# GpSimd's weight split of 128x1024 is four instructions of 128x256 in place of one

## The chip, the cores and the metric

The kernel runs on one core of a Trainium2 chip. The metric is the device time of one launch in microseconds, lower is better. An execution is timed on the device; one more execution is recorded by the hardware profiler, and all profile rows come from that one.

## What is computed

Two layers on 512 tokens of width 1024, all in fp32. Each layer has three parts: a feed-forward block (width 2816), a mixer (sliding-window attention beside an HGRN2 recurrence), and a second feed-forward block. Each part has an RMS norm before it and another behind it, and adds to x.

```python
for layer in range(DEPTH):
    g = norm_gains[layer]
    h = rms_norm(x, g[0])
    x = x + 0.5 * rms_norm(swiglu(h, w_ffn_in[layer, 0], w_ffn_out[layer, 0]), g[1])
    h = rms_norm(x, g[2])
    proj = h @ w_in[layer]
    ...
    y = jnp.concatenate([ya.astype(x.dtype), yh.astype(x.dtype)], axis=-1) @ w_out[layer]
    x = x + rms_norm(y, g[3])
    h = rms_norm(x, g[4])
    x = x + 0.5 * rms_norm(swiglu(h, w_ffn_in[layer, 1], w_ffn_out[layer, 1]), g[5])
```

## The kernel before, in words

Activations lie transposed in SBUF, 8 tiles of 128x512 for the width of 1024. Every product with a weight matrix is made of three matmuls in a reduced fp32 format: both the weight and the activation are split into a high and a low part, and high x high, low activation x high weight and high activation x low weight are added up in PSUM (L667, L668, L669).

The weights come as one stream of chunks, each 128x1024 (eight tiles of 128x128); a layer has 168 of them, and 336 make the program. A chunk passes through four engines, with four slots in each buffer:

1. SyncE copies it from HBM into RAW (L315), once the split of the chunk four before has freed the slot (`w_split`).
2. ScalarE rounds it to WHI (`split_hi`, L429), once TensorE is through with the chunk four before (`w_used`). ScalarE's program has these calls written in between its other work, by hand.
3. GpSimd computes WLO = RAW - WHI (`split_lo`, L350), after a wait for `w_hi` (L349), and raises `w_split`. TensorE waits for `w_split` before the first matmul of the chunk, and SyncE before it fills the RAW slot again.
4. TensorE's `chunk` does 24 matmuls with it.

Eight of the chunks have 512 columns of data, the others 1024. In the feed-forward loops and the down projections `split_lo` is all that GpSimd does. Elsewhere its order is written out:

- At the entry of each part (`pre`, L369): the splits of the first two chunks, then additions of squares for the norm into SS (L378, L380). The third chunk's split comes behind the second addition, the fourth chunk's behind the fourth.
- In each of the four passes of the mixer loop (L396): one split; then, once the cumulative sums BC are ready, five subtractions that make exponents in DD (`exponents`, L360 and L365); the next split; three more exponents; an addition into RP (L407); two more splits. The exponents from the fourth on wait for VectorE's stages (`staged`).

VectorE at an entry does, tile by tile, the scaling of Y (L930), the residual X (L934) and, behind ScalarE's HHI (L446), the low part HLO (L924), then the last additions of squares (L917). In the mixer it does the softmax (L1030 to L1057; L1035 is the row maximum, L1037 and L1039 two small operations behind it), and then the stages: QB and KH, and for each level two multiplications into QC (L1080) and one into KZ (L1081), with copies by mask into SM (L1097, L1101). TensorE's scores wait for each stage. In the feed-forward part it takes two banks (L906, `take`), multiplies them (L989) and makes the low part ULO (L993); ScalarE has Silu (L530) and UHI (L535) in between, and its next two `split_hi` stand behind UHI.

TensorE at an entry works through four output banks at once, tile of h by tile of h (`four`), so that the third chunk serves tiles 4 and 5, the fourth tiles 6 and 7. Behind tile 6 it sums the squares SS over the partitions (L699).

Of the kernel before, what the change touches and what calls it, by code (L numbers as in the profile page):

```python
# [87 lines left out]
HALF = SEQ // 2  # L88
HALVES_OF = [slice(0, HALF), slice(HALF, SEQ)]
SPLIT_TILES = 4  # L90
LAST_SPLIT = 2
EARLY_TILES = 3

INPUT_PARTS = [(k, w) for w in HALVES_OF for k in range(SPLIT_TILES)] + \
    [(k, slice(0, SEQ)) for k in range(SPLIT_TILES, KT)]
XT = len(INPUT_PARTS)
# [42 lines left out]
def build_program(nc, xT, stream, params, sinks, rel_bias, one_hot, masks, out):  # L139
    with ExitStack() as ctx:  # L140
        def sb(name, shape, dt=F32, scope=ctx):
            return scope.enter_context(nc.sbuf_tensor(name, shape, dt))

        def sem(name):
            return ctx.enter_context(nc.semaphore(name))
# [4 lines left out]
        RAW = sb("RAW", [P, RAW_SLOTS, CW])  # L150
        WHI = sb("WHI", [P, SPLIT_SLOTS, CW], F32R)
        WLO = sb("WLO", [P, SPLIT_SLOTS, CW], F32R)
# [62 lines left out]
        w_split = sem("w_split")  # L215
# [73 lines left out]
        def _(sp):  # L289
# [26 lines left out]
            for n, k in enumerate(LAST_ORDER):  # L316
                sp.wait_ge(x_ready, XT * (3 * DEPTH) + LAST_SPLIT + n + 1)
                sp.dma_start(out[:, k, :], X[:, k, :]).then_inc(stored, 16)
# [4 lines left out]
        def _(pool):  # L323
# [21 lines left out]
            def split_lo(L, c, i=0, per=0, cols=CW):  # L345

                n = c % RAW_SLOTS

                pool.wait_ge(w_hi, L * LAYER_CHUNKS + i * per + (c + 1))  # L349
                pool.tensor_tensor(WLO[:, n, 0:cols], RAW[:, n, 0:cols], WHI[:, n, 0:cols], ALU.subtract)\  # L350
                    .then_inc(w_split, 1)

            def exponents(n, it):

# [14 lines left out]
            def pre(L, s, c0):  # L369

                split_lo(L, c0)
                split_lo(L, c0 + 1)
                for k in range(1, POOL_SQ):
                    if k > 1:
                        pool.drain()  # L375
                    pool.wait_ge(sq_done, L * LAYER_SQ + (Q_PRE[s] + k + 1))
                    if k == 1:
                        pool.tensor_tensor(SS[:], SQ[:, 0, :], SQ[:, 1, :], ALU.add).then_inc(sq_free, 2)  # L378
                    else:
                        pool.tensor_tensor(SS[:], SS[:], SQ[:, k % 2, :], ALU.add).then_inc(sq_free, 1)  # L380
                    if k in (2, 4):
                        split_lo(L, c0 + k // 2 + 1)
# [37 lines left out]
        def _(act):  # L420
            def split_hi(L, c, i=0, per=0, cols=CW):

                n = c % RAW_SLOTS
                assert per % RAW_SLOTS == 0

                act.wait_ge(w_dma[n], (L * (LAYER_CHUNKS // RAW_SLOTS) + i * (per // RAW_SLOTS) + (c // RAW_SLOTS + 1)) * 16)

                act.wait_ge(w_used, L * LAYER_CHUNKS + i * per + (c + 1))
                act.activation(WHI[:, n, 0:cols], RAW[:, n, 0:cols], ACT.Copy).then_inc(w_hi, 1)  # L429
# [12 lines left out]
            def high(L, s, p):  # L442

                k, w = INPUT_PARTS[p]
                act.wait_ge(x_ready, (L * 3 + s) * XT + (p + 1))
                act.activation(HHI[:, k, w], X[:, k, w], ACT.Copy,  # L446
                               scale=cur[:, P_GAIN + 2 * s * KT:][:, k:k + 1]).then_inc(h_hi, 1)

            def pre(L, s, c0, cols=CW):

                if s == 0:
                    split_hi(L, c0)
                    act.wait_ge(cur_ready, L + 1)
                    for p in range(2 * SPLIT_TILES):
                        high(L, s, p)
                        if p % 2 == 0 and p < 6:
                            split_hi(L, c0 + p // 2 + 1)
                squared = 0
                for k in range(SPLIT_TILES, KT):
                    high(L, s, k + SPLIT_TILES)  # L460
                    for _ in range(min(3, k - squared)):
                        square(L, Q_PRE[s] + squared, X[:, squared, :])
                        squared += 1
                    if k == SPLIT_TILES and s > 0:
                        split_hi(L, c0 + 3)
# [431 lines left out]
        def _(dve):  # L897
# [29 lines left out]
            def scaled(s, k, w=slice(0, SEQ)):  # L927

                gain = cur[:, P_GAIN + (2 * s - 1) * KT:] if s > 0 else out_gain[:]
                dve.scalar_tensor_tensor(out=Y[:, k, w], in0=Y[:, k, w], scalar=gain[:, k:k + 1],  # L930
                                         in1=RP[:, w], op0=ALU.mult, op1=ALU.mult)

            def residual(k, w=slice(0, SEQ)):
                dve.tensor_tensor(X[:, k, w], X[:, k, w], Y[:, k, w], ALU.add).then_inc(x_ready, 1)  # L934

            def take_last():

                dve.tensor_copy(Y[:, KT - 1, HALVES_OF[1]], bank[6][:, 0:HALF]).then_inc(proj_free, 1)
# [257 lines left out]
            for n, w in enumerate(HALVES_OF):  # L1196
                dve.wait_ge(post_r, 3 * DEPTH * 2 + n + 1)
                if n == 1:
                    take_last()
                for k in range(LAST_SPLIT):  # L1200
                    scaled(0, k, w)
                dve.drain()
                for k in range(LAST_SPLIT):
                    residual(k, w)
            for k in LAST_ORDER[LAST_SPLIT:]:
                if k in POOL_TILES:
# [105 lines left out]
```

## Time and profile before

| | us |
|---|---|
| median of 3 runs | 2141.57 (2140.95 to 2141.94) |
| the profiled execution, its own time | 2142.22 |
| its span | 2140.3 |
| TensorE matmul busy | 1992.0 (93%) |
| GpSimd busy | 927.8 (43%), of it 801.8 in L350 |
| VectorE busy | 871.4 (41%) |
| ScalarE busy | 731.4 (34%) |
| mean granted TensorE clock | 0.981 of full |

The span runs from the first to the last recorded instruction; the device time has 1.9 us around it. PE is TensorE's matmuls, DVE is VectorE, ACT ScalarE, POOL GpSimd. A row of a timeline gives the start, the duration, the engine, the line, the operation with its output and inputs, and how many instructions are merged into it; a bracket gives the idle time before it on its engine and what ended it.

### The profile page before, as it was taken

To read this page: it belongs to the slowest core of one execution; us is meant where nothing else is said; L and a number is where in the kernel's file an instruction comes from. 1 tells how busy PE (TensorE), PEld (TensorE's weight loads), DVE (VectorE), ACT (ScalarE), POOL (GpSimd) and SP (SyncE) were. 2 spreads that over 40 slices of the span, in tenths; PEclk is the share of its full clock that TensorE was granted. 3 is DMA by queue.
4 is the path that set the end of the run, shared out by engine and by line. 5 is a ranking of instruction groups with operands and counts; after the bars stand their busy time and mean duration, and the time that the engine had idled before them with its cause. 6 is when DMAs were issued, how large, how long until landed. Compare 5 with 4: busy or idle time off the path is not lost.

```text
span 2140.3 us, 28594 instructions
## 1 busy us (share of the span) xinstructions
PE 1992.0 (93%) x9946; PEld 1630.0 (76%) x9946; DVE 871.4 (41%) x1253; ACT 731.4 (34%) x1044; POOL 927.8 (43%) x455
## 2 busy tenths in 40 slices
PE   5999999888889899999979999998888889999997
PEld 4888888776658688888768888887666677888886
DVE  7322210587785622210172222017777855222102
ACT  4322222444543422232242223224444444222321
POOL 4444444343443444444344444444344334444452
PEclk9999999999999999999989999999999999999998
DMA  4322233121112222323213222322111113232331
GB/s 147 108 92 94 97 100 117 58 83 39 49 39 79 79 98 98 98 95 112 70 60 110 96 95 91 118 91 96 44 47 49 49 60 98 98 98 98 98 108 50
DMA packets 52041, 182.26 MB, mean 85 GB/s; under 512 B 6248, under 2 KB 7304, under 8 KB 51976
## 3 DMA queue, kind: packets, MB, share of 16 engines
q1 hardware_dynamic: 51976, 181.38, 25.6%
q8 instruction: 42, 0.69, 0.1%
q14 instruction: 23, 0.19, 0.0%
HBM read 178.87 MB, written 2.49 MB: 85 GB/s over the span
## 4 chain that ended last, share of the span: by engine, by line
PE 70%; DVE 11%; issue 8%; DVEq 4%; ACT 3%; POOL 2%; POOLq 1%; ACTq 1%; DMA 0%; SPq 0%
PE bank L667 22%; PE bank L669 22%; PE bank L668 22%; DVE QC L1080 2%; POOL WLO L350 2%; DVE HLO L924 1%; POOLq L375 1%; DVEq L1092 1%; PE bank L875 1%; DVE KZ L1081 1%; ACT HHI L446 1%; DVEq L948 1%; DVE SM L1097 1%; PE bank L877 1%; ACT WHI L429 1%
## 5 line engine op out<-in xcount | busy, mean ns | idle before, releaser
L350 POOL TENSOR_TENSOR WLO<-RAW,WHI 128x1024 fp32r<-128x1024 f32 (+1 forms) x336 | 801.8, 2405 | 1046.6 <-ACT WHI L429 1046.5
L667 PE MATMUL bank<-HHI,WHI 128*128 128x512 f32 (+1 forms) x2000 | 780.8, 390 | 67.3 <-POOL WLO L350 40.7
L668 PE MATMUL bank<-HLO,WHI 128*128 128x512 f32 (+1 forms) x2000 | 763.8, 382 | 0.0
L669 PE MATMUL bank<-HHI,WLO 128*128 128x512 f32 (+1 forms) x2000 | 763.1, 382 | 0.0
L667 PEld LDWEIGHTS bank<-HHI,WHI 128*128 128x128 f32 x2000 | 382.8, 191 | 151.9 <-POOL WLO L350 54.8
L669 PEld LDWEIGHTS bank<-HHI,WLO 128*128 128x128 f32 x2000 | 382.3, 191 | 71.9
L668 PEld LDWEIGHTS bank<-HLO,WHI 128*128 128x128 f32 x2000 | 383.2, 192 | 69.5 <-issue 1.7
L429 ACT ACTIVATE WHI<-RAW 128x1024 fp32r<-128x1024 f32 (+1 forms) x336 | 337.9, 1038 | 67.6 <-PE bank L669 66.9
L667 PE MATMUL bank<-UHI,WHI 128*128 128x512 f32 (+1 forms) x792 | 294.3, 372 | 0.0
L669 PE MATMUL bank<-UHI,WLO 128*128 128x512 f32 (+1 forms) x792 | 292.9, 370 | 0.0
L668 PE MATMUL bank<-ULO,WHI 128*128 128x512 f32 (+1 forms) x792 | 292.8, 370 | 0.0
L535 ACT ACTIVATE UHI<-UB 128x512 f32 (+1 forms) x88 | 55.8, 634 | 466.0 <-DVE UB L989 466.0
L906 DVE TENSOR_TENSOR UB<-bank,R 128x512 f32<-128x512 f32 x88 | 60.8, 691 | 364.0 <-PE bank L669 364.0
L907 DVE COPY Y<-bank 128x512 f32<-128x512 f32 x42 | 29.0, 690 | 386.0 <-PE bank L669 386.0
L668 PEld LDWEIGHTS bank<-ULO,WHI 128*128 128x128 f32 x792 | 148.8, 188 | 28.5
L667 PEld LDWEIGHTS bank<-UHI,WHI 128*128 128x128 f32 x792 | 148.8, 188 | 28.4
L669 PEld LDWEIGHTS bank<-UHI,WLO 128*128 128x128 f32 x792 | 148.8, 188 | 28.1
L906 DVE TENSOR_TENSOR TMP<-bank,R 128x512 f32<-128x512 f32 x88 | 60.9, 692 | 180.6 <-PE bank L669 167.4
L484 ACT ACTIVATE SQ<-Y 128x512 f32<-128x512 f32 x42 | 26.6, 633 | 295.8 <-DVE Y L907 295.8
L530 ACT ACTIVATE TMP<-TMP 128x512 f32<-128x512 f32 x88 | 55.6, 632 | 152.4 <-DVE TMP L906 152.4
L993 DVE TENSOR_TENSOR ULO<-UB,UHI 128x512 f32 (+1 forms) x88 | 63.4, 720 | 80.5 <-ACT UHI L535 80.5
L924 DVE SCALAR_TENSOR_TENSOR HLO<-X,cur,HHI 128x256 fp32r<-128x256 f32 (+1 forms) x72 | 69.8, 970 | 37.4 <-ACT HHI L446 34.8
(171 smaller groups left out, 1362.3 us busy)
## 6 DMA issues: line engine op xcount, KB each, us to landing
RAW<-stream SPq DMA_DIRECT2D x336, 512.0 KB, 3.3
X<-xT SPq DMA_DIRECT2D x4, 512.0 KB, 7.0
yT<-X SPq DMA_DIRECT2D x8, 256.0 KB, 2.0
rel_scratch<-KZ SPq DMA_DIRECT2D x1, 382.0 KB
mask_sb<-masks SPq DMA_DIRECT2D x1, 256.0 KB, 9.9
bias<-rel_scratch SPq DMA_DIRECT2D x2, 128.0 KB
par<-params SPq DMA_DIRECT2D x1, 60.0 KB, 2.4
par<-sinks SPq DMA_DIRECT2D x2, 2.0 KB, 3.5
```

The lines of the kernel that those rows point to most:

```text
L350: pool.tensor_tensor(WLO[:, n, 0:cols], RAW[:, n, 0:cols], WHI[:, n, 0:cols], ALU.subtract)\
L429: act.activation(WHI[:, n, 0:cols], RAW[:, n, 0:cols], ACT.Copy).then_inc(w_hi, 1)
L530: act.activation(TMP[:], TMP[:], ACT.Silu).then_inc(silu_ready, 1)
L535: act.activation(u, UB[:], ACT.Copy).then_inc(u_hi, 1)
L667: pe.matmul(dst, WHI[:, slot, lhs], rhs_hi, start=first, stop=False)
L668: pe.matmul(dst, WHI[:, slot, lhs], rhs_lo, start=False, stop=False)
L669: ins = pe.matmul(dst, WLO[:, slot, lhs], rhs_hi, start=False, stop=last)
L906: return dve.tensor_tensor(dst, src, R[:], ALU.mult)
L907: return dve.tensor_copy(dst, src)
L924: dve.scalar_tensor_tensor(out=HLO[:, k, w], in0=X[:, k, w], scalar=gain[:, k:k + 1], in1=HHI[:, k, w], op0=ALU.mult, op1=ALU.subtract).th ...
L993: dve.tensor_tensor(lo, UB[:], hi, ALU.subtract).then_inc(u_lo, 1)
L1080: dve.tensor_tensor(packed, cut(q), cut(e), ALU.mult)
```

## The change

`split_lo` issues one subtraction for every 256 columns, four for a chunk of 1024 and two for one of 512. The wait ahead of them is the same, and the last of them raises `w_split`.

```diff
 SPLIT_TILES = 4
+SPLIT_PIECE = 256
 LAST_SPLIT = 2
...
                 pool.wait_ge(w_hi, L * LAYER_CHUNKS + i * per + (c + 1))
-                pool.tensor_tensor(WLO[:, n, 0:cols], RAW[:, n, 0:cols], WHI[:, n, 0:cols], ALU.subtract)\
-                    .then_inc(w_split, 1)
+                for at in range(0, cols, SPLIT_PIECE):
+                    part = slice(at, at + SPLIT_PIECE)
+                    ins = pool.tensor_tensor(WLO[:, n, part], RAW[:, n, part], WHI[:, n, part], ALU.subtract)
+                ins.then_inc(w_split, 1)
```

## Rows read from the trace of the kernel before

**Rows 1.** The page, busy time and share of each engine.
```profile
PE 1992.0 (93%) x9946; PEld 1630.0 (76%) x9946; DVE 871.4 (41%) x1253; ACT 731.4 (34%) x1044; POOL 927.8 (43%) x455
```

**Rows 2.** The list of waits: total us, times, longest us.
```profile
PE bank L667 <- POOL WLO L350: 40.7, 10, 6.9
```

**Rows 3.** The timeline of PE: start us, us; in brackets the idle time before.
```profile
46.94 1.13 PE L699 MATMUL bank<-SS,ones 128*128 128x512 f32 x2 [0.29 <-DVE SS L917]
...
706.19 0.79 PE L667 MATMUL bank<-HHI,WHI 128*128 128x512 f32 x1 [6.51 <-POOL WLO L350]
...
717.58 0.70 PE L699 MATMUL bank<-SS,ones 128*128 128x512 f32 x1 [1.31 <-DVE SS L917]
...
733.36 0.50 PE L667 MATMUL bank<-HHI,WHI 128*128 128x512 f32 x1 [1.00 <-POOL WLO L350]
```

**Rows 4.** L350 by shape, by minimum, median and maximum, and in steady feed-forward.
```profile
L350 POOL TENSOR_TENSOR WLO<-RAW,WHI 128x1024 fp32r<-128x1024 f32 x328 | 791.2, 2431 | 1032.8 <-ACT WHI L429 1032.6
...
L350 POOL TENSOR_TENSOR WLO<-RAW,WHI 128x512 fp32r<-128x512 f32 x8 | 10.6, 1346 | 13.8 <-ACT WHI L429 13.8
...
L350 POOL TENSOR_TENSOR WLO<-RAW,WHI x336: 1289/2402/2947, 10.9 to 2109.8; 128x1024 fp32r<-128x1024 f32 x164, 128x512 fp32r<-128x512 f32 x4
...
110.30 4.77 POOL L350 TENSOR_TENSOR WLO<-RAW,WHI 128x1024 fp32r<-128x1024 f32 x2 [6.17 <-ACT WHI L429]
...
117.77 0.69 DVE L906 TENSOR_TENSOR UB<-bank,R 128x512 f32<-128x512 f32 x1 [4.75 <-PE bank L669]
```

**Rows 5.** The timeline of the mixer's second pass, POOL and DVE beside each other.
```profile
500.82 2.08 POOL L365 TENSOR_TENSOR DD<-BC 128x512 f32<-128x512 f32 x2
...
504.65 2.71 POOL L365 TENSOR_TENSOR DD<-BC 128x512 f32<-128x512 f32 x2 [1.76 <-DVE QB L1065]
...
500.92 0.97 DVE L1053 TENSOR_TENSOR small<-small,S 128x8 f32<-128x8 f32 x1
...
505.10 2.55 DVE L1080 TENSOR_TENSOR QC<-PROJ,DD 64x256 f32<-64x256 f32 x2
```

**Rows 6.** The same pass, the split and the stages behind it.
```profile
507.39 2.49 POOL L350 TENSOR_TENSOR WLO<-RAW,WHI 128x1024 fp32r<-128x1024 f32 x1
...
510.24 1.16 POOL L365 TENSOR_TENSOR DD<-BC 128x512 f32<-128x512 f32 x1 [0.36 <-DVE KZ L1081]
...
507.66 2.50 DVE L1081 TENSOR_TENSOR KZ<-KK,DD 128x256 f32<-128x256 f32 x1
...
510.08 1.59 DVE L1080 TENSOR_TENSOR QC<-PROJ,DD 64x256 f32<-64x256 f32 x2
...
513.64 0.42 DVE L1081 TENSOR_TENSOR KZ<-KK,DD 128x256 f32<-128x256 f32 x1
```

**Rows 7.** The third pass, a split and the row maximum.
```profile
542.21 2.40 POOL L350 TENSOR_TENSOR WLO<-RAW,WHI 128x1024 fp32r<-128x1024 f32 x1 [4.76 <-ACT WHI L429]
...
544.15 0.49 DVE L1037 TENSOR_SCALAR small<-small,cur 128x8 f32<-128x8 f32 x1 [0.18 <-issue]
...
544.72 0.23 DVE L1039 TENSOR_SCALAR S<-small,cur 128x8 f32<-128x8 f32 x1
```

**Rows 8.** Entry of the last part of layer 0, its first split.
```profile
683.68 2.59 POOL L350 TENSOR_TENSOR WLO<-RAW,WHI 128x1024 fp32r<-128x1024 f32 x1 [7.82 <-ACT WHI L429]
...
684.25 2.31 DVE L924 SCALAR_TENSOR_TENSOR HLO<-X,cur,HHI 128x256 fp32r<-128x256 f32 x1 [0.18 <-ACT HHI L446]
...
687.48 0.48 DVE L924 SCALAR_TENSOR_TENSOR HLO<-X,cur,HHI 128x256 fp32r<-128x256 f32 x1 [0.19 <-ACT HHI L446]
```

**Rows 9.** The same entry, the third chunk's split.
```profile
703.79 2.35 POOL L350 TENSOR_TENSOR WLO<-RAW,WHI 128x1024 fp32r<-128x1024 f32 x1
...
704.08 2.60 DVE L924 SCALAR_TENSOR_TENSOR HLO<-X,cur,HHI 128x512 fp32r<-128x512 f32 x1 [1.71 <-ACT HHI L446]
```

**Rows 10.** The same part, before its seventh chunk.
```profile
722.59 2.40 POOL L350 TENSOR_TENSOR WLO<-RAW,WHI 128x1024 fp32r<-128x1024 f32 x1 [2.63 <-ACT WHI L429]
...
723.07 2.46 DVE L989 TENSOR_TENSOR UB<-UB,TMP 128x512 f32<-128x512 f32 x1 [1.52 <-ACT TMP L530]
```

## The prediction

> **What bounds the kernel now.** I first read the busy shares: TensorE works in 93% of the span and GpSimd in 43% [rows 1], so GpSimd has room on average and only places count. GpSimd itself waits 1032.6 us for ScalarE's half of the split (WHI, L429) [rows 4]: most of its 336 splits could not begin sooner. Then the list of waits [rows 2]: TensorE waits for a split (WLO, L350) in only ten places, 40.7 us together. The timeline of TensorE shows which ones [rows 3]: six are the entries of the three parts of each layer, where the third chunk's split is queued on GpSimd behind two additions of squares (6.51 us in the row at 706.19), and four are the seventh chunk of each feed-forward part, 1.00 us in the row at 733.36. Elsewhere TensorE's gaps are in the mixer, where VectorE's stages are late.
>
> Last, the durations of VectorE beside those of GpSimd, and this is the view that matters. A VectorE instruction that reads two tensors from SBUF does not run while a GpSimd subtraction runs: KZ, asked for at 507.66, takes 2.50 us and ends 0.28 us after the split that began at 507.39 [rows 6]; the same form takes 0.42 at 513.64, where no split runs. HLO at 684.25 takes 2.31 and ends 0.29 after its split [rows 8], and the later HLO of the same shape takes 0.48. Each waits for the whole GpSimd instruction. At the border between two GpSimd instructions that wait for nothing, VectorE does get in: the 8-element addition at 500.92 takes 0.97 and ends with the first of the two subtractions, while the second is right behind [rows 5]. GpSimd gets in between two VectorE instructions in the same way: the two QC multiplications at 505.10 take 2.55 beside two subtractions [rows 5].
>
> **What one split costs after the change.** It adds three instructions to each of 328 splits of 1024 columns and one to each of 8 of 512. Nothing moves, no wait is added, and the semaphore rises with the last piece. The trace has no 256-column piece. The shortest split of 512 columns takes 1.289 us and the median of 1024 takes 2.402 [rows 4], so a fixed part of 2 x 1.289 - 2.402 = 0.18 and a piece of 0.73. Two splits in a row take 4.77, not 4.80 [rows 4], so the next begins some 0.03 us before the end of the last: four pieces take about 2.84, 0.44 us more. Lower bound: nothing more. Upper bound, by the means that include collisions (1.346 and 2.431): 0.26 fixed, 0.8 us more. I take 0.44, since the shortest rows are free of collisions.
>
> By the Trainium skill (GPSIMD Engine Reference, 3.1 Elementwise) a TENSOR_TENSOR of 2048 fp32 columns takes 4497 ns; with the 2402 of 1024 columns that would make the fixed part 0.31 us and a split 0.92 us longer, an estimate from the page, by which this would come out slower (rival 2). No row here has 2048 columns.
>
> In steady feed-forward nothing of this is seen: the pair at 110.30 is for the chunks after the one that TensorE ends at 117.77 [rows 4], 5 us behind the first of the pair's ends. A chunk lasts 5.44 (4.75 + 0.69 between two takes of VectorE), and the DMA into the freed RAW slot, issued up to 0.44 later, has four chunks to land in. If that cover were gone, 270 feed-forward splits at 0.44 would be 120 us.
>
> **The mixer, 8 passes.** With the piece as the unit, a GpSimd piece and a VectorE operation alternate. The QC pair gives the handover: 2.55 / 2 = 1.28 for one subtraction of 1.04 with one multiplication, so 0.24 over the subtraction. A piece and one multiplication then take 0.70 + 0.24 = 0.94. Before, KZ and the next three operations (QC, QC, KZ) ended at 512.1 (510.08 + 1.59 + 0.42) [rows 6]. After, the four lie behind four pieces: 507.4 + 4 x 0.94 = 511.2, so 0.9 earlier. But GpSimd's next subtraction (one of the exponents, L365), which used to run at 510.24 inside those operations, now runs inside the next stage together with the one after it: 2 x 1.28 + 0.42 = 3.0 there in place of 1.95. That ends at 514.2, where it ended at 514.06. The wait isn't removed, it is dealt out in four portions, and the relief is paid back two operations later. With the handover at 0.16 instead it would be 0.2 us earlier; with 0.3, 0.3 later. I take 0. The stage and the masks behind it follow without slack, so a shift here is one of the whole pass.
>
> The other split that touches VectorE's chain ends at 544.61, and the row max at 544.15 waits for it to 544.64 [rows 7]. Four pieces end at 545.05. The max gets in after the third, at 544.35, but the small operation behind it (544.72, ending at 544.95) would now wait for the last piece, to 545.08: +0.13, between 0 and the whole 0.44. Eight passes: +1.0 us, between -2 and +6.
>
> **The entries, 6.** Early collision [rows 8]: HLO waits for the first piece alone and ends at 684.9 rather than 686.6. The residual, the scaling and the next HLO each wait for one piece; that HLO ends near 687.6 where it ended at 687.96. The gain is the gaps in which VectorE waited for ScalarE anyhow, about 0.4 us: -2.4 for six.
>
> Third chunk [rows 9]: VectorE has its 512-column operations ready one after the other, so three get in between the pieces. HLO at 704.08 ended 0.54 after its split, so each of them costs GpSimd between 0 and 0.54; GpSimd starts somewhat before VectorE's record ends, and I take 0.42. Before, the split ended at 706.14; after, 703.79 + 4 x 0.72 + 3 x 0.42 = 707.9, so TensorE starts 1.8 later. Behind it TensorE has 36 matmuls and then waits for VectorE's sum of squares, 1.31 us at 717.58 and 0.29 at 46.94 [rows 3]. VectorE is now earlier, so this wait goes. I let it take up 1.1 in the four entries of the first kind and 0.5 in the two that open a layer, near those rows: 4 x 0.7 + 2 x 1.3 = +5.4.
>
> Seventh chunk of the four feed-forward parts: the product UB at 723.07 waits for a split to 725.5 [rows 10]. The split began at 722.59; after one piece, at 723.3, the product would end near 723.9, 1.7 earlier, and with it ScalarE's UHI and the WHI that the late split waits for. Less 0.44 for the split itself this is over 1.0, so the stall at 733.36 goes: 4 x -1.05 = -4.2.
>
> **Sum.** +1.0 - 2.4 + 5.4 - 4.2 = -0.2 us. The profiled execution took 2142.22 us (span 2140.3), 0.65 over the median of 2141.57. From the median: 2141.4. A measurement of this kernel tells about 0.2%, 4.3 us, from no change.
>
> **Rivals.**
> Relief (faster): VectorE's long waits in fact shrink to one piece because the following operations don't meet GpSimd again, or GpSimd gives way. Then 2.50 - 0.9 = 1.6 us in each of eight passes and six early entries: about -22 us, 2120 at full strength, and near 2130 if half of it is paid back. For it: VectorE is what TensorE waits for in the mixer. Against it: QC at 510.08 met the very next subtraction and ended, with its pair, 0.27 after that one did (511.67 against 511.40). The Trainium skill (SBUF — State Buffer, Who interferes with whom) says that the shared port is held for the whole instruction and the loser fully blocks; read alone, shorter instructions give this rival, and the trace agrees on the block, with 2.50 us for 0.42.
> Dear pieces (slower): each GpSimd instruction costs more than 0.18, so that the last piece, on which TensorE and VectorE wait, is later. It decides at the split of 507.39 and the third chunk of each entry. At the upper bound a split is longer by 0.8, 0.36 over what I take: two splits in eight passes 5.8, the entries, most of it absorbed, 1. Then 2148. For it the means in rows 4, against it the shortest row. By the estimate from the Trainium skill's 4497 ns (GPSIMD Engine Reference, 3.1) it would be 0.48 a split over what I take, 2150.
> GpSimd keeps the port (the change does not split what it is meant to): VectorE isn't let in between pieces, which wait for nothing. Then every collision is 0.44 longer: 8 x 0.6, six early 2.6, third chunk 0.44 x 6 less what is absorbed, about +8, 2150. Against it stands the row at 500.92.
>
> **Chances.** The exchange as worked out 0.62, its own range 2136 to 2146 (0.10 of it faster by over 0.2%, 0.05 slower); relief 0.14; dear pieces 0.16 (0.13 over the bound); port kept 0.08. So faster 0.24, same 0.50, slower 0.26. The range for 8 in 10 takes in the dear pieces and the half-paid relief in part: 2133 to 2149.
>
> **What would show it.** Right: four WLO rows of 0.70 to 0.75 us a split, stretched to about 1 beside VectorE; no KZ or HLO over 1.2 us but more of them at 0.8; TensorE's wait at the third chunk 1.5 to 2 us longer, the one ahead of the sum of squares and the one of 1.1 in the feed-forward gone; a mixer pass as long as before within 0.3 us. Wrong: VectorE operations of 2.5 us left (port kept), pieces of 0.8 and more alone (dear), or a pass shorter by 1 us (relief).

## The result and the profile after

| | before | after |
|---|---|---|
| median of 13 runs each, us | 2141.57 (2140.41 to 2142.11) | 2146.23 (2144.58 to 2147.51) |
| ratio, 95% interval | | 1.0023 [1.0014, 1.0031] |
| the profiled execution, its span | 2142.22, 2140.3 | 2146.64, 2144.7 |
| its mean granted TensorE clock | 0.981 | 0.970 |

The change makes the kernel 4.7 us slower, 0.22%. I had predicted 2141.4, no change. The measured time is inside the range and just past the bound of 4.3 us, so the forecast missed its side. With the three added lines L350 is now L353, L667 to L669 are L670 to L672, and so on.

The page after, busy time and the split's group, against [rows 1, 4]:

```profile
PE 2003.1 (93%) x9946; PEld 1642.3 (77%) x9946; DVE 841.0 (39%) x1253; ACT 731.0 (34%) x1044; POOL 1103.8 (51%) x1447
...
L353 POOL TENSOR_TENSOR WLO<-RAW,WHI 128x256 fp32r<-128x256 f32 x1328 | 977.9, 774 | 896.3 <-ACT WHI L432 896.1
```

The list of waits after, against [rows 2] (us in total, times, longest):

```profile
PE bank L670 <- POOL WLO L353: 63.5, 13, 9.2
```

GpSimd has 176 us more work, and a piece takes 774 ns on average. The list gives 22.8 us more of waits for splits. But 15.6 of them are two waits, at 14.35 (6.36 us) and 1077.19 (9.24), that stood before in about the same length against VectorE's HLO (6.95 at 15.01 and 8.59 at 1074.90). So some 7 us are new, and the program is 4.7 us longer.

The timeline after, mixer passes two and three, against [rows 6, 7]:

```profile
509.15 3.47 POOL L353 TENSOR_TENSOR WLO<-RAW,WHI 128x256 fp32r<-128x256 f32 x4
...
512.58 2.40 POOL L368 TENSOR_TENSOR DD<-BC 128x512 f32<-128x512 f32 x2
...
509.42 0.87 DVE L1084 TENSOR_TENSOR KZ<-KK,DD 128x256 f32<-128x256 f32 x1
...
510.21 1.81 DVE L1083 TENSOR_TENSOR QC<-PROJ,DD 64x256 f32<-64x256 f32 x2
...
512.04 0.86 DVE L1084 TENSOR_TENSOR KZ<-KK,DD 128x256 f32<-128x256 f32 x1
...
512.83 2.44 DVE L1083 TENSOR_TENSOR QC<-PROJ,DD 64x256 f32<-64x256 f32 x2
...
543.83 2.83 POOL L353 TENSOR_TENSOR WLO<-RAW,WHI 128x256 fp32r<-128x256 f32 x4 [4.34 <-ACT WHI L432]
...
545.77 0.23 DVE L1040 TENSOR_SCALAR small<-small,cur 128x8 f32<-128x8 f32 x1 [0.18 <-issue]
...
546.08 0.61 DVE L1042 TENSOR_SCALAR S<-small,cur 128x8 f32<-128x8 f32 x1
```

Four pieces alone take 2.83 (543.83), beside VectorE 3.47 (509.15). KZ takes 0.87 instead of 2.50, but the next QC pair now spans 1.81 us instead of 1.59, the second KZ 0.86 instead of 0.42, and the pair at 512.83 takes 2.44 beside two exponents, where it took 1.59 beside one (at 512.03). That is the exchange which I had worked out.

The timeline after, the entry of layer 0's last part, its seventh chunk, and one row of the mixer part's entry, against [rows 3, 8 to 10]:

```profile
685.96 0.69 DVE L927 SCALAR_TENSOR_TENSOR HLO<-X,cur,HHI 128x256 fp32r<-128x256 f32 x1 [0.18 <-ACT HHI L449]
...
705.07 4.12 POOL L353 TENSOR_TENSOR WLO<-RAW,WHI 128x256 fp32r<-128x256 f32 x4
...
705.36 0.98 DVE L927 SCALAR_TENSOR_TENSOR HLO<-X,cur,HHI 128x512 fp32r<-128x512 f32 x1 [1.70 <-ACT HHI L449]
...
706.26 1.21 DVE L937 TENSOR_TENSOR X<-X,Y 128x512 f32<-128x512 f32 x1
...
709.24 0.80 PE L670 MATMUL bank<-HHI,WHI 128*128 128x512 f32 x1 [8.27 <-POOL WLO L353]
...
720.09 1.02 PE L702 MATMUL bank<-SS,ones 128*128 128x512 f32 x2
...
725.46 0.81 DVE L992 TENSOR_TENSOR UB<-UB,TMP 128x512 f32<-128x512 f32 x1 [1.51 <-ACT TMP L533]
...
735.01 0.50 PE L670 MATMUL bank<-HHI,WHI 128*128 128x512 f32 x1 [0.25 <-POOL WLO L353]
...
422.75 0.50 PE L670 MATMUL bank<-HHI,WHI 128*128 128x512 f32 x1 [0.85 <-POOL WLO L353]
```

HLO takes 0.69 at the first split, not 2.31. The third chunk's pieces take 4.12 and TensorE waits 8.27 for them, not 6.51. UB takes 0.81, not 2.46, and the seventh chunk's wait is 0.25, not 1.00. The last row is new: the fourth chunk, too, is late now in that entry, by 0.85.

To see where the time comes from, here are the starts of the same TensorE instruction in both kernels (from the timelines; the shift is after less before, us):

| place | before | after | shift |
|---|---|---|---|
| seventh chunk, first part | 63.04 | 63.15 | +0.11 |
| first mixer pass, layer 0 | 456.48 | 457.42 | +0.94 |
| second pass | 504.10 | 505.87 | +1.77 |
| entry of the last part | 685.49 | 687.20 | +1.71 |
| its third chunk | 706.19 | 709.24 | +3.05 |
| its sum of squares | 717.58 | 720.09 | +2.51 |
| its seventh chunk | 733.36 | 735.01 | +1.65 |
| seventh chunk, layer 1 | 1123.33 | 1125.07 | +1.74 |
| first mixer pass, layer 1 | 1516.80 | 1519.58 | +2.78 |
| fourth pass, near its end | 1695.55 | 1699.05 | +3.50 |
| entry of the last part | 1744.59 | 1749.06 | +4.47 |
| its seventh chunk | 1792.46 | 1796.87 | +4.41 |

There are two kinds of step. At the mixer parts' entries 0.8 and 1.0 are lost; at the feed-forward entries, counted up to the seventh chunk, nothing (+0.11, -0.06, +0.09, -0.06). Together this is +1.9. The rest is +0.8 in the first pass of layer 0, +0.7 late in layer 1's mixer and +1.0 in the down projection after it. In those stretches the granted clock falls: it is 0.93 in the first pass (1.00 before), 0.89 in the last pass of layer 1 (1.00) and 0.73 in the first 10 us of the down projection (0.83).

### The profile page after: what moved, and what is told of

Same layout as the page of the kernel before. It is cut to its first block, busy times and chain, and to the rows that moved or that the text cites. A ratio compares the mean times of both kernels' runs of the same rounds, so it can differ in the third digit from the quotient of the medians.

```text
span 2144.7 us, 29586 instructions
## 1 busy us (share of the span) xinstructions
PE 2003.1 (93%) x9946; PEld 1642.3 (77%) x9946; DVE 841.0 (39%) x1253; ACT 731.0 (34%) x1044; POOL 1103.8 (51%) x1447
## 4 chain that ended last, share of the span: by engine, by line
PE 72%; DVE 10%; issue 5%; POOL 4%; DVEq 3%; ACT 3%; POOLq 1%; ACTq 1%; DMA 0%; SPq 0%
PE bank L670 23%; PE bank L671 23%; PE bank L672 23%; POOL WLO L353 4%; DVE QC L1083 2%; PE bank L878 1%; POOLq L378 1%; DVE KZ L1084 1%; PE bank L802 1%; DVEq L951 1%; DVE HLO L927 1%; DVEq L1095 1%; PE bank L880 1%; DVE Y L933 1%; ACT HHI L449 1%
## 5 line engine op out<-in xcount | busy, mean ns | idle before, releaser
L353 POOL TENSOR_TENSOR WLO<-RAW,WHI 128x256 fp32r<-128x256 f32 x1328 | 977.9, 774 | 896.3 <-ACT WHI L432 896.1
L670 PE MATMUL bank<-HHI,WHI 128*128 128x512 f32 (+1 forms) x2000 | 783.4, 392 | 73.3 <-POOL WLO L353 63.5
L672 PE MATMUL bank<-HHI,WLO 128*128 128x512 f32 (+1 forms) x2000 | 765.0, 383 | 0.0
L670 PEld LDWEIGHTS bank<-HHI,WHI 128*128 128x128 f32 x2000 | 384.6, 192 | 157.9 <-POOL WLO L353 68.6
L672 PEld LDWEIGHTS bank<-HHI,WLO 128*128 128x128 f32 x2000 | 383.9, 192 | 72.4
L670 PE MATMUL bank<-UHI,WHI 128*128 128x512 f32 (+1 forms) x792 | 294.3, 372 | 0.0
L672 PE MATMUL bank<-UHI,WLO 128*128 128x512 f32 (+1 forms) x792 | 292.9, 370 | 0.0
L670 PEld LDWEIGHTS bank<-UHI,WHI 128*128 128x128 f32 x792 | 148.8, 188 | 28.5
L672 PEld LDWEIGHTS bank<-UHI,WLO 128*128 128x128 f32 x792 | 148.8, 188 | 28.0
L802 PE MATMUL bank<-QC,KZ 128*128 128x128 f32 (+1 forms) x384 | 61.5, 311 | 24.7 <-DVE ST L1116 15.4
```

Of the source, the lines that this page charges most:

```text
L353: ins = pool.tensor_tensor(WLO[:, n, part], RAW[:, n, part], WHI[:, n, part], ALU.subtract)
L670: pe.matmul(dst, WHI[:, slot, lhs], rhs_hi, start=first, stop=False)
L672: ins = pe.matmul(dst, WLO[:, slot, lhs], rhs_hi, start=False, stop=last)
L802: ins = pe.matmul(bank[b + l % 2][0:keys, c * P:c * P + P], KZ[:, l, c * P:c * P + keys], QC[:, l % QC_SLOTS, c, :, :].rearrange("p h q -> ...
```

## The experiments

Each median stands beside that of the kernel before, measured with it; intervals are at 95%. The medians of the table rest on 8 to 11 runs each, but that of the third split alone on 6 and the last two on 5. In the experiments on places, `split_lo` gets a parameter, and the calls differ only in it:

```diff
-            def split_lo(L, c, i=0, per=0, cols=CW):
+            def split_lo(L, c, i=0, per=0, cols=CW, piece=CW):
...
-                for at in range(0, cols, SPLIT_PIECE):
-                    part = slice(at, at + SPLIT_PIECE)
+                for at in range(0, cols, min(piece, cols)):
+                    part = slice(at, at + min(piece, cols))
```

| which splits are in pieces | us | before | ratio |
|---|---|---|---|
| the four of each entry | 2146.30 | 2141.82 | 1.0023 [1.0014, 1.0033] |
| the four of each mixer pass | 2145.86 | 2141.82 | 1.0019 [1.0010, 1.0028] |
| all others | 2138.47 | 2141.82 | 0.9986 [0.9977, 0.9995] |
| these, and the entries' first two | 2135.44 | 2141.82 | 0.9972 [0.9961, 0.9982] |
| the entries' first two | 2139.44 | 2141.66 | 0.9989 [0.9980, 0.9998] |
| the entries' third | 2148.47 | 2141.66 | 1.0033 [1.0021, 1.0045] |
| the entries' fourth | 2139.26 | 2141.66 | 0.9990 [0.9981, 0.9999] |
| in a pass, the one between exponents | 2144.78 | 2141.66 | 1.0016 [1.0007, 1.0025] |
| in a pass, the one before exponents | 2142.54 | 2141.66 | 1.0004 [0.9995, 1.0013] |
| all, in halves of 512 | 2139.35 | 2141.66 | 0.9991 [0.9982, 1.0000] |
| all but the third and the mixer loop | 2131.46 | 2141.91 | 0.9955 [0.9942, 0.9969] |
| all but the third | 2133.52 | 2141.57 | 0.9960 [0.9946, 0.9975] |

### By place: entries, mixer, the rest

```diff
-                split_lo(L, c0)
-                split_lo(L, c0 + 1)
+                split_lo(L, c0, piece=SPLIT_PIECE)
+                split_lo(L, c0 + 1, piece=SPLIT_PIECE)
...
+                    split_lo(L, c0 + k // 2 + 1, piece=SPLIT_PIECE)
```

> Four pieces only in the four splits of each part's entry; all other splits are whole. Theory A (entries: the third and fourth chunk's splits let VectorE in between their pieces, each later by 1.8 us, and this is not absorbed any more): the two mixer entries cost 1.0 us each, the four feed-forward entries 0.3 to 0.7 each, since the relief at the seventh chunk is missing: 2.5 to 5 us over the kernel before, granted clock as before, 0.98. Theory B (the clock: nearly all of the loss is TensorE at half clock in the mixer passes): 0 to 1 us over before, clock 0.98. Theory C (0.42 us more per split wherever one is waited for): 12 splits at 0.42, 5 us.

The second has it in the four calls of the mixer loop alone:

```diff
-                    split_lo(L, C_GROUPS + 2, t, 4)
+                    split_lo(L, C_GROUPS + 2, t, 4, piece=SPLIT_PIECE)
```

> Four pieces only in the 32 splits of the mixer loop. Theory A: the passes stay at 47.6 us, 0 over the kernel before, clock 0.98. Theory B: 2 to 3 us over, mean granted clock 0.97, and windows at 0.5 behind the wait of 1.93 us ahead of the third scores. Theory C: two splits a pass, 16 x 0.42 = 6.7 us over.

The third has it in the feed-forward loops, the down projections and between the parts:

```diff
-                    split_lo(L, c0 + n, i, RAW_SLOTS)
+                    split_lo(L, c0 + n, i, RAW_SLOTS, piece=SPLIT_PIECE)
```

> Four pieces in all splits but those of the entries and of the mixer loop. Theories A and B: faster than the kernel before, by 4 us (the wait of 1.0 us at the seventh chunk of four feed-forward parts goes, because the split of the sixth chunk no longer holds up the product UB), so 2137.5. Theory C: no gain, 0 to 1 us over, as steady splits are hidden.

Measured: +4.5, +4.0 and -3.4 us. They add up to +5.2 where the whole change gives +4.7. My sum had +3.0 for the four splits of the entries, +1.0 for the mixer and -4.2 for the rest. So both costs are larger than I had them, and the gain at the seventh chunk is real: 0.84 us for each of four parts, where I had taken 1.05. By the wait itself it is 0.75 (1.00 became 0.25).

### The four splits of an entry, one by one

Two calls of `pre` in pieces, added to the third kernel above:

> As e3_rest, and the first two splits of each entry in pieces too; the third and fourth of an entry and the mixer loop whole. Theories A and B: 4 us from the seventh chunk and 0.4 for each of six first collisions, 6 us under the kernel before, 2135.5. Theory C: at or above the kernel before, since six to twelve more splits are longer.

and then by themselves:

> Four pieces only in the first two splits of each entry. Theory A: the relief of VectorE's first collisions alone, 0.4 us in each of six entries: 2.4 us under the kernel before, 2139.3. Theory C (longer splits cost): 0 to 2 us over it.

Only the third split:

```diff
-                    split_lo(L, c0 + k // 2 + 1)
+                    split_lo(L, c0 + k // 2 + 1, piece=SPLIT_PIECE if k == 2 else CW)
```

> Four pieces only in the third split of each entry, the one that TensorE stands waiting for, with three VectorE operations between the pieces. Theory A: it ends 1.8 us later, and the wait for the sum of squares behind it takes up 0.3 to 1.3 of that: 0.5 us in four entries and 1.3 in two, 3 to 6 us over the kernel before. If the sum of squares takes it up wholly: 0. Theory C: 0.42 x 6 less what is taken up, 0 to 1 us.

Only the fourth (`k == 4`):

> Four pieces only in the fourth split of each entry. It ends 1 to 1.7 us later but still before TensorE needs it, since the third is not late: theory A 0 us, at most 1 over the kernel before; if it alone makes the new wait of 0.85 us ahead of tile 6, 3 to 5 us over. Theory C: 0 to 1.

The third split alone costs 6.8 us, 1.1 an entry, more than the 3 to 6 expected. The first two give 2.2, as worked out (0.4 each entry). The fourth gives 2.4, which I hadn't counted at all. Its timeline, at the entry of layer 0's mixer part (GpSimd's third and fourth split, VectorE beside the fourth):

```profile
410.34 2.34 POOL L353 TENSOR_TENSOR WLO<-RAW,WHI 128x1024 fp32r<-128x1024 f32 x1
...
416.03 4.16 POOL L353 TENSOR_TENSOR WLO<-RAW,WHI 128x256 fp32r<-128x256 f32 x4
...
416.76 1.00 DVE L927 SCALAR_TENSOR_TENSOR HLO<-X,cur,HHI 128x512 fp32r<-128x512 f32 x1
...
417.68 1.22 DVE L937 TENSOR_TENSOR X<-X,Y 128x512 f32<-128x512 f32 x1
```

HLO takes 1.00 beside a piece, and X behind it 1.22, where a whole split holds such an operation 2.6 us, as it did at 704.08 [rows 9]. VectorE is on the way to the sum of squares here, on which TensorE waits in the kernel before: in this kernel that wait is at most 0.04 in all six entries.

Alone, these splits give +6.8, -2.2 and -2.4, which add up to +2.2, but all four of an entry in pieces cost +4.5 (the first row of the table). In that kernel TensorE waits for the fourth chunk as well, 0.35 to 0.62 us in four of the six entries, for instance:

```profile
44.99 0.50 PE L670 MATMUL bank<-HHI,WHI 128*128 128x512 f32 x1 [0.62 <-POOL WLO L353]
```

So a fourth split in pieces helps while the third is on time. Behind a third that is late its gain is gone, and TensorE waits for its end in some entries.

Then everything in pieces but the third split and the mixer loop:

```diff
-                split_lo(L, c0)
+                split_lo(L, c0, piece=SPLIT_PIECE)
...
+                    split_lo(L, c0 + k // 2 + 1, piece=CW if k == 2 else SPLIT_PIECE)
...
+                    split_lo(L, c0 + n, i, RAW_SLOTS, piece=SPLIT_PIECE)
```

> Four pieces in all splits but the third of each entry and those of the mixer loop. If the third alone is at fault: e4_all_but_34 (2135.4) less the 2.4 us that e11_fourth gained: 2133. If third and fourth are bound together: 2135 to 2138.

and the kernel after with nothing else changed than that split, whole again:

> The changed kernel with the third split of each entry whole. By e1, e9 and e11 the third split's pieces cost 9 us among the others: 2137, with the clock of the mixer still at fault.

Its timeline at the entry that stands above for the kernel after:

```profile
701.99 2.35 POOL L353 TENSOR_TENSOR WLO<-RAW,WHI 128x1024 fp32r<-128x1024 f32 x1
...
704.39 0.79 PE L670 MATMUL bank<-HHI,WHI 128*128 128x512 f32 x1 [6.50 <-POOL WLO L353]
...
729.98 0.50 PE L670 MATMUL bank<-HHI,WHI 128*128 128x512 f32 x1 [0.26 <-POOL WLO L353]
```

Keeping that one split whole takes 12.7 us off the kernel after, 2.1 an entry; I had expected 9. Of these 1.77 are the shorter wait (6.50 for 8.27). The rest is in the stretch behind it. From the third chunk's first matmul to the sum of squares TensorE took, in the six entries (from the start of L670 to that of L702, before L667 and L699):

| | us |
|---|---|
| before | 10.76, 11.34, 11.39, 10.95, 11.39, 11.37 |
| after | 10.65, 10.81, 10.85, 10.67, 11.05, 10.85 |
| after, third split whole | 10.35, 10.55, 10.56, 10.58, 10.56, 10.56 |

The difference between the first two rows is what absorbs the 1.77, and it is 0.39 an entry (the sums are 67.20 and 64.87), not the 1.1 and 0.5 that I took. The windows of the entry at 706 say why. Each gives the stretch and its length, PE's busy time with its instructions, the granted clock, the DMA share and GB/s. Before:

```profile
706.00:708.00 2.00, 1.81 (x4) 0.50 0.39 104
...
708.00:710.00 2.00, 2.00 (x7) 0.62 0.41 158
...
710.00:712.00 2.00, 2.00 (x11) 1.00 0.00 0
```

After:

```profile
709.00:711.00 2.00, 1.76 (x4) 0.50 0.33 63
...
711.00:713.00 2.00, 2.00 (x6) 0.50 0.50 199
...
713.00:715.00 2.00, 2.00 (x7) 0.59 0.00 0
...
715.00:717.00 2.00, 2.00 (x10) 1.00 0.00 0
```

Behind its wait TensorE starts at the lower clock, 0.50, which is 1.2 GHz, and stays there for 7 matmuls of 0.63 us before, for 12 after. Each is some 0.2 slower than at full clock, so from the first to the last of 36 matmuls' starts it takes 9.69 us in the one and 10.62 in the other. The number of matmuls at the lower clock varies by entry in both kernels, 7 to 13 and 6 to 13, 62 and 63 in all, so the change doesn't set it. But the wait of 1.31 for the sum of squares [rows 3] belonged to an entry with 7. At 1765.30, with 13, it was 0.21, in a stretch of the same length (11.37). The waits of the six entries before are 0.29, 0.04, 1.31, 0.00, 1.12 and 0.21 us, 2.97 in all. I had let them take up 5.4. What I had read as slack was TensorE's own time in four of the six entries.

In the entries with few matmuls at the lower clock something else took the room. In the kernel after, the one with 6 is the entry with the wait of 0.85 for the fourth chunk. In the kernel with pieces in the four splits of each entry, the four waits for the fourth chunk stand in the entries with 6 to 8 of them, and all six stretches take 10.63 to 10.83. With the third split alone in pieces, the stretch with 6 of them goes down to 9.62.

### The two mixer splits that touch VectorE

```diff
-                    split_lo(L, C_GROUPS + 3, t, 4)
+                    split_lo(L, C_GROUPS + 3, t, 4, piece=SPLIT_PIECE)
```

> Four pieces only in the split that stands between the exponents of the mixer loop (8 splits). Theory B: this one makes the wait of 1.93 us, so the whole loss of e2_mixer but 1 us is here: 2.5 to 3.5 us over the kernel before, mean clock 0.972. Theory C: 0.42 each, 3.4 us, with the clock at 0.98. The clock tells them apart.

The same in the call of `C_GROUPS + 2`:

> Four pieces only in the split ahead of the exponents of the mixer loop (8 splits), the one that ends beside the row maximum. Both theories: 0.1 us a pass by the profile, 0.8 to 1.0 us over the kernel before, clock 0.98; Theory C: 3.4 us.

Timelines: GpSimd's split, and the starts of the second and the third pass on TensorE. The split between exponents in pieces:

```profile
507.12 3.48 POOL L353 TENSOR_TENSOR WLO<-RAW,WHI 128x256 fp32r<-128x256 f32 x4
...
503.84 1.09 PE L831 MATMUL bank<-ident,S 128*128 128x128 f32 x8 [1.17 <-DVE S L1060]
...
551.33 1.09 PE L831 MATMUL bank<-ident,S 128*128 128x128 f32 x8 [1.21 <-DVE S L1060]
```

The one ahead of the exponents in pieces:

```profile
507.62 2.50 POOL L353 TENSOR_TENSOR WLO<-RAW,WHI 128x1024 fp32r<-128x1024 f32 x1
...
504.34 1.09 PE L831 MATMUL bank<-ident,S 128*128 128x128 f32 x8 [1.32 <-DVE S L1060]
...
552.14 1.09 PE L831 MATMUL bank<-ident,S 128*128 128x128 f32 x8 [1.33 <-DVE S L1060]
```

A pass of the first is 47.49 us, of the second 47.80, before 47.62. So the pieces between exponents gain 0.13, and the others lose 0.18 in layer 0 and 0.10 in layer 1, where a pass takes 47.72 at full clock. In this the longer way through the small operations behind the row maximum shows: the wait for S is 1.32, before 1.22. Together this is nearly nothing, as forecast. But the first kernel is 3.1 us slower than before and not 1 faster: its passes of 47.5 stand beside others of 48.2 to 48.4 (1516.81 to 1565.20), in which the clock falls. Another 1.1 us are lost in the down projection behind them, where the granted clock is 0.71 in the first 10 us (0.83 before).

### The clock in the mixer

After, the granted clock in the first two passes, then in steps of 2 us (busy time of PE, PEld, DVE, ACT and POOL, then PEclk, DMA share, GB/s):

```profile
456.00:506.00 50.00, 45.08 (x288) 34.56 (x287) 38.48 (x59) 21.60 (x38) 23.07 (x26) 0.93 0.13 43
...
504.00:554.00 50.00, 42.58 (x290) 32.23 (x289) 39.31 (x60) 21.99 (x40) 23.49 (x26) 1.00 0.12 42
...
467.00:469.00 2.00, 0.63 (x5) 0.66 (x6) 1.81 (x6) 0.32 (x2) 1.66 (x2) 0.97 0.01 2
...
469.00:471.00 2.00, 1.29 (x6) 1.03 (x6) 1.90 (x3) 0.00 (x0) 0.79 (x1) 0.50 0.00 0
...
471.00:473.00 2.00, 2.00 (x10) 1.90 (x10) 1.90 (x5) 0.00 (x0) 0.00 (x0) 0.50 0.00 0
```

Before:

```profile
456.00:506.00 50.00, 43.42 (x298) 33.39 (x297) 39.31 (x61) 22.85 (x41) 21.90 (x14) 1.00 0.13 43
...
504.00:554.00 50.00, 43.68 (x301) 33.52 (x303) 39.32 (x60) 23.23 (x42) 22.28 (x15) 1.00 0.13 42
```

TensorE's timeline before, then after:

```profile
462.69 0.95 PE L799 MATMUL bank<-QC,KZ 128*64 128x128 f32 x7 [1.61 <-DVE KZ L1081]
...
467.56 1.13 PE L799 MATMUL bank<-QC,KZ 128*128 128x128 f32 x8 [0.97 <-DVE ST L1113]
```

```profile
462.45 0.95 PE L802 MATMUL bank<-QC,KZ 128*64 128x128 f32 x7 [0.44 <-ACT Y L608]
...
468.37 1.58 PE L802 MATMUL bank<-QC,KZ 128*128 128x128 f32 x8 [1.93 <-DVE ST L1116]
...
470.65 2.05 PE L802 MATMUL bank<-QC,KZ 128*128 128x128 f32 x8 [0.71 <-DVE KZ L1084]
...
516.81 1.13 PE L802 MATMUL bank<-QC,KZ 128*128 128x128 f32 x8 [1.93 <-DVE ST L1116]
```

The clock drops to 0.50 behind a stretch in which TensorE had little to do: it waits 1.93 us ahead of the third scores of the pass, at 468.37. Before, the wait ahead of them was 0.97 (467.56), and one of 1.61 stood ahead of the first scores (462.69), where 0.44 is left. This is the exchange of the mixer as TensorE sees it: the pass stays as long, but 1 us of waiting moves from one wait into the next one, which becomes twice as long. The eight matmuls at 470.65 take 2.05 where they take 1.13 at full clock; the wait of 0.71 ahead of them is short only since the scores before them ran slowly too (1.16 in the second pass, and 1.15 before). In the second pass the same wait of 1.93 (516.81) isn't followed by a fall.

I first moved some of TensorE's work so that this wait gets shorter, in the kernel after and in the kernel before:

```diff
                     next_group(2, 7, 8)
+                    next_group(3, 0, 2)
                     scores(2)
                     scores(3)
-                    next_group(3, 0, 2)
```

> The changed kernel, with the two tiles of the next group that stand behind TensorE's fourth scores moved ahead of its third, so that its wait of 1.93 us there becomes one of 0.6 us, and a wait of about 1.5 us appears behind the fourth scores. The chain through VectorE stays as it is. Theory B (the loss in the mixer is half clock behind the longer wait): no windows of 20 us under 0.9 at the passes, first pass back to 47.6 us, 2 to 3 us under the changed kernel, 2143.5. Theory C (longer splits alone): no change, 2146.

> The same move in the kernel before, as the control: the clock is full in its passes already, so all theories expect 2141.5 to 2142.5, at most 0.1 us a pass for scores that begin later.

2147.76 against 2141.66, ratio 1.0031 [1.0019, 1.0043], and 2144.45, 1.0014 [1.0005, 1.0023]: both are worse, and neither is what I expected. In the first, the profiled execution (2146.30, the lowest of six) has full clock and 47.6 us in the first three passes of each layer, and 0.88 in the last pass of layer 1, much as the kernel after; why the other five took up to 2150.82 isn't shown. In the second, which has no piece at all, the wait ahead of the third scores went, the one ahead of the fifth grew from 0.28 to 1.65, and in two passes, of 49.4 us each, the clock fell there:

```profile
520.18 2.05 PE L799 MATMUL bank<-QC,KZ 128*128 128x128 f32 x8 [1.65 <-DVE KZ L1081]
```

So the clock can fall by the pattern of waits alone, without a piece. Then I kept the order and gave TensorE something to do in the wait, a matmul that nothing uses, in the kernel with pieces in the mixer loop alone:

```diff
                     next_group(2, 7, 8)
+                    bank_free(L, J_GROUPS + 3, t, 4)
+                    pe.matmul(bank[3][:, 0:512], ones[:], X[:, 0, 0:512], start=True, stop=True)
                     scores(2)
```

> e2_mixer with one fp32 matmul of 128x512, 1.1 us, of which nothing is used, in TensorE's wait of 1.93 us ahead of the third scores. Theory B (clock): the stretches at half clock in the passes become rarer, mean clock 0.975 to 0.98, 2142 to 2144 in place of 2145.9. If the clock isn't the cause: 2145.9 or above, as an added matmul can't speed the chain.

The kernel before with the same line at 256 columns, as the control:

> The control: the kernel before with one such matmul of 128x256, 0.6 us, in the wait of 0.98 us at the same place. All theories: 2141.0 to 2142.0, as the clock is full there already and the wait covers it.

2141.45 with it, ratio 0.9999 [0.9990, 1.0008], where the pieces without it had 2145.86; the control 2141.67, 1.0000 [0.9991, 1.0009]. Windows of the first pass, and the timeline of the second:

```profile
456.00:506.00 50.00, 44.31 (x300) 33.69 (x299) 39.31 (x61) 22.82 (x41) 24.18 (x26) 1.00 0.13 43
```

```profile
512.97 1.02 PE L864 MATMUL bank<-X,ones 128*128 128x512 f32 x2
...
515.06 1.13 PE L802 MATMUL bank<-QC,KZ 128*128 128x128 f32 x8 [1.07 <-DVE ST L1118]
```

The clock of the first pass is 1.00 again (0.93 without the matmul), and the wait that was 1.93 is 1.07. So the 4.0 us that the pieces in the mixer cost go with the clock; every pass of the kernel with the matmul takes 47.6 (47.59 to 47.62). In the whole change, and with the best set of places (its mixer split between exponents also in pieces):

> The changed kernel as it is, with the unused matmul of 128x512 in TensorE's wait of 1.93 us. If the clock in the mixer is what the prediction lacked: 4 us under the changed kernel, 2142, mean clock 0.98. If the loss is the entries: 2145 to 2146.

> e13_all_but_3 with four pieces in the split between the exponents of the mixer too, and the unused matmul of e14 in TensorE's wait. Theory B: the 0.15 us a pass that e7_ahead1 showed between its slow stretches is kept, 1 us under e13, 2132. If the clock isn't held: 2 to 3 us over e13.

The kernel after with the matmul takes 2143.57, 1.0011 [1.0002, 1.0020]: 2.7 us are given back where I had expected 4, and the 2.0 that stay agree with the +1.9 of the entries. With the best set it is 2131.84, 0.9953 [0.9939, 0.9966], the same as without either (2131.46).

### Halves

`SPLIT_PIECE = 512` in the kernel after:

> All splits in two pieces of 512 in place of four of 256: 0.14 us more for a split in place of 0.42, and fewer turns for VectorE. Theory A: the third split lets in one or two operations in place of three, 0.6 to 1 us later rather than 1.8, all of it taken up by the wait for the sum of squares; the relief at the seventh chunk stays in part (the product UB waits 1.3 us rather than 2.2 or 0.5): 2 to 4 us under the kernel before. The mixer: by theory B the clock decides, -1 to +3 us. Together 2138 to 2144. Theory C: a third of the loss of the changed kernel, 2143.

2139.35, 0.9991 [0.9982, 1.0000]. GpSimd at the third chunk:

```profile
702.83 2.93 POOL L353 TENSOR_TENSOR WLO<-RAW,WHI 128x512 fp32r<-128x512 f32 x2
```

Two halves take 2.93 there, 0.58 more than the whole. One operation of VectorE gets in between them, where three get in between four pieces; TensorE waits 7.09. The seventh chunk's wait is 0.38, so that gain is kept.

## Why the prediction was wrong

**What held.** A piece 0.73 and a split 0.44 longer: 2.83 for four, against 2.40. Splits of the steady feed-forward hidden: the third kernel, with most of them in pieces, is faster. HLO and KZ down to 0.69 and 0.87. The exchange in the mixer at nothing: passes of 47.6 before and after wherever the clock stays up. The +0.13 behind the row maximum: the wait for S grew by 0.11. (The operation at 544.15 that the prediction calls the row maximum is the first of the two small ones behind it, L1037; the sum isn't touched.) The first collisions -0.4 an entry: -2.2 us by themselves. The third chunk +1.8: 8.27 less 6.51 is 1.76.

**The step that failed first** is the absorption behind the third chunk, "1.1 in the four entries of the first kind and 0.5 in the two that open a layer". The starts give 0.39 an entry, 2.3 us in all, not 5.4. I took the idle time of one row as slack of four entries; with TensorE's restart at the lower clock, which varies from entry to entry, the six had 2.97 us of it in all. By the starts, the third chunk is 7.7 us later over the six entries (8.4 forecast, 6 x 1.8 less 2.4), the stretch behind it takes up 2.3 (5.4), and the way to the seventh chunk 3.4 (4.2). So my -1.2 for the entries became +1.9, and 3.1 of this difference is the absorption; the other two misses cancel.

**The term that is missing** is TensorE's clock in the mixer. No step of the prediction priced it, because each wait that I shifted there was counted as time only. The exchange itself came out as forecast, and with it the wait ahead of the third scores went from 0.97 to 1.93. The clock makes about 2.5 us of the 4.7, by the starts, and 2.7 by the kernel with the unused matmul. Why it falls in some passes only stays open.

**The gain not counted** is the fourth split, 2.4 us alone. In the kernel after it is not to be seen: with the third chunk 1.8 later TensorE no longer waits for the sum of squares in any entry, with the fourth split whole or in pieces. With the third whole the gain comes back: 2135.4 became 2131.5 when the fourth was cut too.

**The rivals.** Relief fell: the pass is no shorter. Port kept fell with the first KZ of 0.87. The sentence of the Trainium skill (SBUF — State Buffer, Who interferes with whom) that the loser is blocked for the other's whole instruction agrees with both kernels: KZ's 2.50 us behind a whole split became 0.87 behind a piece. The rival failed because the operations behind KZ met a piece or an exponent each. Dear pieces, the rival on the side that came true, fell in its mechanism: four pieces cost 0.43 more than one instruction, 0.14 for each of the three added, where I had taken 0.44 in all. By the 4497 ns of the Trainium skill (GPSIMD Engine Reference, 3.1 Elementwise) I had estimated 0.31 for each; the measured 2.83 decides against it.

## What to carry to other kernels

Cut a long GpSimd instruction only where VectorE, behind it, is what the others wait for; leave whole the one whose end TensorE stands waiting for. Here that one split of six entries costs 12.7 us beside the others, which gain 8.1 without it, and the kernel with every split but this and the mixer's in pieces beats both, 2131.5 us, 10.4 less than before. And before counting an idle time of TensorE as slack, look at the same wait in every entry and at the clock ahead of it: the 1.31 us of one entry were 0.04 in another, where more matmuls ran at the lower clock. Last, a pass that stays as long can still cost time if its waits are dealt out anew, because one that grows can let the clock fall.

## What the runs showed that I had not expected

With a wait that had grown from 0.97 to 1.93 us TensorE's clock fell in some mixer passes and not in others with the same waits; what tells those passes apart wasn't tried and stays open. One unused matmul of 1.02 us in that wait held the clock and gave back 4.4 us, and one of half its columns cost nothing in the kernel before.

GpSimd's pieces and VectorE's operations take turns one by one: four pieces of 0.71 beside three VectorE operations took 4.12, so 0.43 for each operation that got in, whose own row shows 0.98 and 1.21.
